# 24 V rows weighted by ScalarE and added by GpSimd, the gate round six rows later, and twelve slots for the last V rows

## What is computed

```
q = (h @ w_q).reshape(b, s, 8, 2, 128);  scores = einsum('bshpd,hpnd->bshpn', q, sub_keys)
top_s, top_i = top_k(scores, 16)                 # per half; then the best 16 of 16 x 16 sums
gates = softmax(best_s)                           # 16 per head and token
act = gelu(einsum('td,ted->te', xt, u_tab[it]))   # 128 chosen rows of U per token
out = einsum('te,ted->td', gt * act, v_tab[it])   # 128 chosen rows of V per token
x   = layer_norm(alpha * h + out)
```

## Time and profile before

| | us |
|---|---|
| median of 3 runs (lowest to highest) | 1466.14 (1464.67 to 1469.86) |
| the profiled execution | 1468.57 |
| its span in the profile | 1466.6 |
| PE busy | 1367.8 (93%) |
| DVE busy | 1144.3 (78%) |
| POOL busy | 663.7 (45%) |
| ACT busy | 397.9 (27%) |
| all DMA | 444.26 MB, mean 303 GB/s |

### The profile page before, as it was taken

One profiled execution on the slowest core, in us unless ns is written; L12 is line 12 of the kernel. 1 busy time (PEld: TensorE's weight loads), 2 busy tenths in 40 slices (PEclk: granted clock), 3 DMA queues, 4 the chain that ended last, 5 costly groups with the idle time before them and its releaser, 6 DMA issues.

```text
span 1466.6 us, 18813 instructions
## 1 busy us (share of the span) xinstructions
PE 1367.8 (93%) x6494; PEld 957.1 (65%) x6494; DVE 1144.3 (78%) x2495; ACT 397.9 (27%) x815; POOL 663.7 (45%) x548
## 2 busy tenths in 40 slices
PE   8999989799999999989999599999999999999943
PEld 6787755488888888867544255578888854444411
DVE  4837266678888888789889998878999887666786
ACT  4224000512120101269410055566551010000020
POOL 2334111353333345620335565645445565666673
PEclk9999999999999999999999799999999999999986
DMA  6411234577878889982599999999899999999996
GB/s 237 151 59 58 91 139 144 187 239 235 314 268 310 291 308 414 414 333 77 185 390 397 401 381 413 403 353 398 336 363 353 414 413 414 414 414 414 412 328 257
DMA packets 118429, 444.26 MB, mean 303 GB/s; under 512 B 11712, under 2 KB 24512, under 8 KB 101952
## 3 DMA queue, kind: packets, MB, share of 16 engines
q0 software_dynamic: 73728, 268.47, 48.1%
q1 hardware_dynamic: 44032, 173.56, 30.9%
q10 hardware_dynamic: 576, 1.05, 0.2%
HBM read 440.94 MB, written 2.10 MB: 302 GB/s over the span
## 4 chain that ended last, share of the span: by engine, by line
DVE 32%; PE 30%; DMA 16%; POOL 7%; issue 6%; DVEq 5%; ACT 4%; ACTq 1%; SPq 0%
DMA big<-in_peer_v_dram,idx 11%; DVE y L1200 8%; PE ps L1441 7%; PE ps L1387 7%; DVE big L1177 7%; PE ps L1370 6%; DMA big<-in_peer_u_dram,idx 4%; POOL big L618 4%; POOL big L606 3%; PE ps L1534 2%; PE ps L1625 2%; DVE work L1060 2%; ACT wr L668 1%; DVE topi L1059 1%; DVE top L1062 1%
## 5 line engine op out<-in xcount | busy, mean ns | idle before, releaser
L606 POOL DMA_INDIRECT big<-in_peer_u_dram,idx x256 | 311.9, 1218 | 537.3 <-DVE dots L1177 430.0
L1177 DVE CUSTOM_DVE_ANT_0 big<-big,xh 128x1024 f32<-128x1024 f32 x256 | 311.7, 1224 | 64.5 <-DMA big<-in_peer_u_dram,idx 42.4
L1200 DVE SCALAR_TENSOR_TENSOR y<-big,wgt,y 128x1024 f32<-128x1024 f32 x245 | 314.1, 1282 | 48.9 <-DMA big<-in_peer_v_dram,idx 45.4
L618 POOL DMA_INDIRECT big<-in_peer_v_dram,idx x256 | 290.7, 1136 | 108.2 <-issue 67.1
L1441 PE MATMUL ps<-big,pool_mem 128*128 128x512 f32 x512 | 224.3, 593 | 0.0
L1370 PE MATMUL ps<-xT,big 128*128 128x256 f32 x960 | 211.1, 380 | 0.0
L1370 PEld LDWEIGHTS ps<-xT,big 128*128 128x128 f32 x960 | 181.7, 190 | 24.3
L1441 PEld LDWEIGHTS ps<-big,pool_mem 128*128 128x128 f32 x512 | 96.7, 190 | 118.6 <-issue 118.6
L1441 PE MATMUL ps<-y,pool_mem 128*128 128x512 f32 x256 | 114.8, 599 | 0.0
L1441 PE MATMUL ps<-xT,pool_mem 128*128 128x512 f32 x256 | 113.5, 593 | 0.0
L1370 PE MATMUL ps<-xT,y 128*128 128x256 f32 x480 | 106.4, 380 | 0.0
(11 more groups left out here) (253 smaller groups left out, 1587.9 us busy)
## 6 DMA issues: line engine op xcount, KB each, us to landing
big<-u_pairs_dram SPq DMA_DIRECT2D x32, 1024.0 KB, 8.0
big<-v_pairs_dram SPq DMA_DIRECT2D x32, 1024.0 KB, 8.0
y<-u_pairs_dram SPq DMA_DIRECT2D x16, 1024.0 KB, 7.9
xT<-u_pairs_dram SPq DMA_DIRECT2D x16, 1024.0 KB, 8.1
y<-v_pairs_dram SPq DMA_DIRECT2D x16, 1024.0 KB, 7.9
xT<-v_pairs_dram SPq DMA_DIRECT2D x16, 1024.0 KB, 8.1
big<-in_w_in_dram SPq DMA_DIRECT2D x24, 512.0 KB, 5.8
pool_mem<-in_peer_w_q_dram SPq DMA_DIRECT2D x12, 1024.0 KB, 7.6
```

Source lines behind the costliest of these rows:

```text
L606: nc.gpsimd.indirect_dma_start(urow[n % RING], None, peer_u2, bass.IndirectOffsetOnAxis(ap=idx[:, u, e:e + 1], axis=0)).then_inc(s_u[n % R ...
L618: nc.gpsimd.indirect_dma_start(vrow[n % RING], None, peer_v2, bass.IndirectOffsetOnAxis(ap=idx[:, u, e:e + 1], axis=0)).then_inc(s_v[n % R ...
L1177: V.tensor_tensor_reduce(out=urow[n % RING], in0=urow[n % RING], in1=xh[:, u // PH * D:(u // PH + 1) * D], scale=1.0, scalar=0.0, op0=ALU. ...
L1200: V.scalar_tensor_tensor(acc_rows[t], vrow[n % RING], wgt[:, u % 2, e:e + 1], acc_rows[t], ALU.mult, ALU.add).then_inc(s_vadd, 1)
```

## The change

- The V rows 0 to 23 (`POOL_ROWS`) are no longer added by VectorE. ScalarE multiplies the row in its slot by the weight (job `weighted`), at the place in its list that `weighted_behind(m)` gives: ahead of `act` (0, (4 m - 9) // 5), so rows 0 to 3 ahead of `act` (0, 0) and row 23 ahead of `act` (0, 16). GpSimd adds it to the sum in `acc_rows[1]`, which it has cleared (`pool_add`); in GpSimd's list this stands at n = m + 38, between `gather_u(n)` and `gather_v(n - 32)`. VectorE adds that sum to `acc_rows[0]` at row 124 (`MERGE_ROW`).
- `scale` of tile 1 therefore moves behind `act` (1, 4), ahead of the gelu of unit 8, and VectorE waits for it at row 160.
- The gate round moves from row 84 to row 90, and with it the choices of units 7 to 11 and all teams, by six rows. Unit 12 stays at row 174. The gelu of unit 3 moves from `act` (0, 26) to (0, 23), the gates from (0, 21) to (0, 18).
- From V row 228 on there are twelve slots: the six of `vrow` and the six of `urow`, once all products are done.

```diff
+WIDE_ROWS = 38 * RING
+POOL_ROWS = list(range(24))
+MERGE_ROW = 124
-ROUND_ROW = 84
+ROUND_ROW = 90
-LATER_CHOICES = {ROUND_ROW + 1: 7, ROUND_ROW + 6: 8, ROUND_ROW + 12: 9, ROUND_ROW + 18: 10, ROUND_ROW + 24: 11, ROUND_ROW + 90: 12}
+LATER_CHOICES = {ROUND_ROW + 1: 7, ROUND_ROW + 6: 8, ROUND_ROW + 12: 9, ROUND_ROW + 18: 10, ROUND_ROW + 24: 11, ROUND_ROW + 84: 12}
+def weighted_behind(m):
+    return max(0, (4 * m - 9) // 5)
+def v_slot(n):
+    if n < WIDE_ROWS:
+        return n % RING, n // RING
+    lap, place = divmod(n - WIDE_ROWS, 2 * RING)
+    return (place, WIDE_ROWS // RING + lap) if place < RING else (place, lap)
+def v_turned_out(n):
+    return n - RING if n < WIDE_ROWS + RING else n - 2 * RING
...
-    during = {(0, 2): 1, (0, 12): 2, (0, 26): 3, (1, 4): 8, (1, 11): 9, (1, 20): 10}
+    during = {(0, 2): 1, (0, 12): 2, (0, 23): 3, (1, 4): 8, (1, 11): 9, (1, 20): 10}
+            for m in POOL_ROWS if r == 0 else ():
+                if weighted_behind(m) == n:
+                    jobs.append(("weighted", (m,), None))
             add("act", r, n, by="act" if r == 0 else "dve")
+            if (r, n) == (1, 4):
+                jobs.append(("scale", (1,), None))
-            if (r, n) == (0, 21):
+            if (r, n) == (0, 18):
                 jobs.append(("gates", (), None))
...
-        vrow = [rows[:, 8 + s, :] for s in range(RING)]
+        vrow = [rows[:, 8 + s, :] for s in range(RING)] + urow
...
+            def pool_add(m):
+                if m == 0:
+                    pool.wait_ge(s_h, 2 * GATHERED)
+                    nc.gpsimd.memset(acc_rows[1], 0.0).then_inc(s_pzero, 1)
+                    pool.wait_ge(s_pzero, 1)
+                if m:
+                    pool.wait_ge(s_padd, m)
+                pool.wait_ge(s_weighted, m + 1)
+                nc.gpsimd.tensor_tensor(acc_rows[1], acc_rows[1], vrow[m % RING], ALU.add).then_inc(s_padd, 1)
...
+                place, _ = v_slot(n)
+                out = v_turned_out(n)
+                if WIDE_ROWS + RING <= n < WIDE_ROWS + 2 * RING:
+                    pool.wait_ge(s_dot, ROWS)
+                elif out in TAIL_ROWS:
+                    pool.wait_ge(s_pv, TAIL_ROWS.index(out) + 1)
+                elif out in POOL_ROWS:
+                    pool.wait_ge(s_padd, out + 1)
+                elif out >= 0:
+                    pool.wait_ge(s_vadd, out + 1 - sum(m < out for m in TAIL_ROWS + POOL_ROWS))
...
             for n in range(ROWS + LAG):
                 if n < ROWS:
                     gather_u(n)
+                if n - LAG - RING in POOL_ROWS:
+                    pool_add(n - LAG - RING)
                 if n >= LAG:
                     gather_v(n - LAG)
...
+                if kind == "weighted":
+                    m = arg[0]
+                    act.wait_ge(s_pwgt, m // TOPK + 1)
+                    act.wait_ge(s_v[m % RING], 16 * (1 + m // RING))
+                    A.activation(vrow[m % RING], vrow[m % RING], ACT.Copy,
+                                 scale=wgt[:, m // TOPK, m % TOPK:m % TOPK + 1]).then_inc(s_weighted, 1)
...
                 if e == 0:
+                    if n == PH * TOPK or n == 0:
+                        dve.wait_ge(s_y, t + 1)
+                    if u >= 2 and (u - 2) * TOPK in POOL_ROWS:
+                        dve.wait_ge(s_weighted, min(len(POOL_ROWS), (u - 1) * TOPK))
                     weights(u)
+                if n in POOL_ROWS:
+                    return
...
+                if n == MERGE_ROW:
+                    dve.wait_ge(s_padd, len(POOL_ROWS))
+                    V.tensor_tensor(acc_rows[0], acc_rows[1], acc_rows[0], ALU.add).then_inc(s_merged, 1)
+                    fence()
```

More of the change, by code:

```diff
@@ L179, in static_jobs @@
         add(kind, *arg, by="dve" if kind == "outA" or kind == "out" and arg[0] < GATHERED else "act")
-    for t in range(GATHERED):
-        jobs.append(("scale", (t,), None))
+    jobs.append(("scale", (0,), None))
     for n in range(PH):
@@ L246, in static_jobs @@
     for i, (kind, arg, by) in enumerate(jobs):
-        if kind in ("split", "norm", "scale", "gelu", "gates", "expert", "onehot", "half", "early", "dnorm"):
+        if kind in ("split", "norm", "scale", "gelu", "gates", "expert", "onehot", "half", "early", "dnorm", "weighted"):
             placed.append((kind, arg, by, None, None))
@@ L454, in layer @@
         s_u = [sem(f"urow_gathered{s}") for s in range(RING)]
-        s_v = [sem(f"vrow_gathered{s}") for s in range(RING)]
+        s_v = [sem(f"vrow_gathered{s}") for s in range(2 * RING)]
         s_dot, s_gel, s_vadd = sem("dots_done"), sem("gelu_ready"), sem("vrows_added")
@@ L458, in layer @@
         s_pv = sem("vrow_in_psum")
+        s_pzero, s_pwgt = sem("pool_sum_cleared"), sem("pool_weights_ready")
+        s_weighted = sem("vrow_weighted")
+        s_padd, s_merged = sem("pool_vrows_added"), sem("pool_sum_merged")
         s_blk = [sem(f"blocks_loaded{s}") for s in range(DPAIRS)]
@@ L613, in gather_v @@
                     pool.wait_ge(s_wdone, 8)
[L614 to L618, removed]
+                place, _ = v_slot(n)
[8 more added lines that the diff above has]
+                    pool.wait_ge(s_vadd, out + 1 - sum(m < out for m in TAIL_ROWS + POOL_ROWS))
+                nc.gpsimd.indirect_dma_start(vrow[place], None, peer_v2,
                                              bass.IndirectOffsetOnAxis(ap=idx[:, u, e:e + 1], axis=0)
-                                             ).then_inc(s_v[n % RING], 16)
+                                             ).then_inc(s_v[place], 16)
             for n in range(ROWS + LAG):
@@ L647, in _ @@
                     act.wait_ge(s_h, 2 * t + 2)
+                    if t == 1:
+                        act.wait_ge(s_merged, 1)
                     A.activation(acc_rows[t], xh[:, t * D:(t + 1) * D], ACT.Copy, scale=ALPHA).then_inc(s_y, 1)
@@ L685, in _ @@
                     A.activation(dots[:, u % 4, :], dots[:, u % 4, :], ACT.Gelu).then_inc(s_gel, 1)
+                    continue
+                if kind == "weighted":
[4 more added lines that the diff above has]
+                                 scale=wgt[:, m // TOPK, m % TOPK:m % TOPK + 1]).then_inc(s_weighted, 1)
                     continue
@@ L1412, in _ @@
             for kind, arg, by, b, n in JOBS:
-                if kind in ("split", "norm", "scale", "gelu", "gates", "onehot", "half", "dnorm"):
+                if kind in ("split", "norm", "scale", "gelu", "gates", "onehot", "half", "dnorm", "weighted"):
                     continue
@@ L1641, in _ @@
                 pe.wait_ge(s_diag, k + 1)
-                pe.wait_ge(s_v[m % RING], 16 * (1 + m // RING))
+                place, laps = v_slot(m)
+                pe.wait_ge(s_v[place], 16 * (1 + laps))
                 for half in range(2):
-                    last = T.matmul(ps[:, 4 + half, :], diag[:, k % 4, :], vrow[m % RING][:, half * 512:(half + 1) * 512],
+                    last = T.matmul(ps[:, 4 + half, :], diag[:, k % 4, :], vrow[place][:, half * 512:(half + 1) * 512],
                                     start=(k == 0), stop=(k == len(TAIL_ROWS) - 1))
```

9 lines of the change are left out of this document (5 added, 4 removed).

## The result

The changed kernel takes 1498.21 us (median of 4 runs, 1497.31 to 1499.94), the kernel before 1465.79 (4 runs, 1464.67 to 1469.86): ratio 1.0209, 95% interval 1.0192 to 1.0227. The profiled span is 1498.0 against 1466.6, so 31.4 us longer. The forecast was 1482.5 with a range of 1450 to 1495. Its sign held, and so did most of its order of events; its size was half of what came (16.4 us against 32.4).

The account below looks back on a forecast made before the run. VectorE was taken to pace the rows until about 550 us, then the DMA is full. The sum 1397.9 + 15 + 24 + 46 = 1483 against the span of 1466.6 gives +16.4, on the median 1482.5; range 1450 to 1495.

Parts of the forecast that it names:

- sign: Whole kernel: slower, by 16.4 us; chances slower 0.58, same 0.17, faster 0.25.
- order of events: From rows to tail: round 15 us late, teams 24 us late, then the path behind TensorE's end is longest.
- Part 1: Rows 32 to 55: VectorE loses 33.8 us of additions; GpSimd's list decides, row 62 at 550, 5 us earlier.
- Part 2: Gate round, six rows later: starts 15 us later (bounds -4 and +40), TensorE idles 22 us.
- Part 3: Teams (1, 1, m) meet work left at its row: TensorE waits 10.4, 4.0 and 9.5, sum 24 us.
- Part 4: Tail behind TensorE's last expert: 46 us to the end, now the longest path.
- rival (c): Tail: twelve slots bring nothing, as V row 241 waits for tail row 229; 3.5 us, taken as part of the forecast.
- slack: TensorE's end in the kernel before: 22 us under the span, to absorb 22 of 39 us of delay.
- Rival (a): Rows to the end: the work is really hidden and teams cost nothing, 1448 us; faster, below 1461.7, chance 0.25.
- Rival (b): Lock of GpSimd's additions on VectorE: 47 us against 33.8 saved, row 62 at 568, end at 1495; chance 0.13.

Follow-up runs that it names:

- The first experiment: The changed kernel with tile 0's layer norm, two choices, a gelu and a scale moved clear of teams (1, 1, m): 1479.31 us, ratio 1.0083.
- the first kind of set: Sets of runs in which the kernel before takes 1464 to 1471 us, not about 1498; the change loses 2.1% there.

## Why the prediction was wrong

By its own steps, against the sum 1397.9 + 15 + 24 + 46 = 1483 for the span:

- **Part 1, the step that failed.** GpSimd's list as the limit: `gather_u(62)` at 544, row 62 at 550. They came at 550.18 and 558.08. The start was right (409.83 against 409.8), the addition too (2.42), and the round without waits took 5.25, at the low end of 5.2 to 6.0. What the sum left at nothing was what each addition does to VectorE, 27 us at least in the stretch (33.6 if each instruction is set against the median of its form before), and that GpSimd then stands 14.8 us behind VectorE's products. Its data landed after 5.74 us, as counted, but VectorE began the product 2.2 us later still. The 33.8 us that VectorE was to gain were thus paid back nearly whole, row 62 came 3.7 later from row 32 instead of 5 earlier. The row for it, was read and even priced at 1.97 us by 24; it was put into a rival at 0.13 instead of into the sum. That rival's 47 us were too many, its mechanism was the one at work. Its time, 1495, came near by luck: it had row 62 at 568, 10 us too late, and lacked what TensorE lost behind its pauses and the longer tail.
- **Part 2, six rows: +15.** Measured +21.6 in TensorE's idle time. The six rows alone cost 14.7 with the additions on GpSimd (291.0 against 276.3 from row 32) and 17.9 without (287.2 against 269.3), so the count of gathers and DMA rate was good to 3 us. The other 7.0 (276.3 against 269.3) are what GpSimd's additions cost at row 84; with memsets in their place the round comes 8.0 earlier (283.0).
- **Part 3, teams: 24, in 10.4, 4.0 and 9.5.** Measured 10.17, 3.07 and 7.54, 20.8 in all, at the named teams. Right, and shown by removing it (19 us).
- **Not in the sum: TensorE slow behind a pause.** The last expert ends 48.8 us later than before. From the last `act` of the first half, which ended 0.4 earlier, and 42.5 us of further waits (21.6, 0.1 ahead of the first team, and 20.8) 6.7 are left. Behind the wait of team 6 TensorE falls back by another 1.3 us, behind team 13 by 1.5, behind team 15 by 2.5, and 1.1 behind the first team of the group (1, 0, m); in the stretches of these three waits the granted clock is 0.81, 0.93 and 0.80. Behind the pause ahead of the round nothing more is lost. The first experiment agrees: TensorE's end came 20.4 us earlier, counted from `act` (0, 31), though a new wait of 2.65 stood against the 20.8 taken away.
- **Part 4, tail: 46.** Measured 51.3: 6.1 until the first tail row (5.8 counted), 26.8 for the rows (25.6), 3.4 until the sum (nothing), 15.0 for the rest (14.8). The 3.4 are VectorE's, whose last additions wait for landings, and these are late by V row 241, which needs the slot of tail row 229: no gather starts between 1448.23 and 1456.87, and fifteen are still to come, until 1476.94. The prediction named that wait, under rival (c), as a price of 3.5 us on the transfers, and left it out of the path from TensorE's end. No run takes it away by itself.
- Sum of what was measured: 1397.9 - 0.4 + 21.6 + 20.9 + 6.7 + 51.3 = 1498.0. Against the 1483 no term carries the miss alone: the round 6.6, TensorE behind its pauses 6.7, the tail 5.3, and the teams took 3.1 less than was counted.

That TensorE's end had slack and would become the start of the longest path was right. The slack was smaller than the 22 us counted: with the measured tail it is 1466.6 - 1397.9 - 51.3 = 17.4. The end itself is still released by a transfer, one that waited for TensorE. Rival (a) is refuted: at row 84 the work given to GpSimd doesn't even pay. Rival (b) had the mechanism, but not the size of its term.

## What to carry to other kernels

Before work goes from VectorE to an idle GpSimd, count how many of VectorE's two-input instructions stand beside it, and charge each overlap to VectorE in the sum, not in a rival; only what lies outside them is a gain (seven early additions brought row 62 as early as twelve did, twelve in place of 24 turned a loss into a gain in the first kind of set). When a block of work moves in a fixed list, write down what stays at its place and now falls inside the block. Let a wait of TensorE on the path cost its own length plus the slow restart behind it, here 1.3 to 2.5 us.

## What was not expected of the hardware

- A GpSimd addition of 128 x 1024 held even a VectorE shift of 64 columns with one input: 2452 ns on the mean of two instead of 196 (L1151 against L1095), each ending within 0.1 us of the addition beside it, and still 484 with memsets in its place.
- GpSimd itself was hardly held: 2.35 to 2.82 us for each of its 24 additions, while a product took up to 3.98.
- An addition over 8 columns took 0.21 us in the middle case and up to 1.24.
- TensorE could take 24 to 38 us for one `act` of 32 matmuls, instead of 6.9, without waiting for anything the profile shows. That was in three sets of runs out of six, and in the kernel before as well.
